# One-core layer step: the feed-forward block's weight sums and GpSimd's other arithmetic placed on VectorE

## The chip, the cores and the metric

The kernel runs on one core of one Trainium2 chip. The metric is the device time of one execution in microseconds (us). Engines are named as in the profile: PE is TensorE, DVE is VectorE, ACT is ScalarE, POOL is GpSimd, SP is SyncE (here only a DMA queue).

## The reference

One decoder layer for 512 prompt tokens and 8 sample tokens (T = 520 columns), D_MODEL = 1024, D_FF = 2816, all in 32-bit floats: RMSNorm, an input projection, an mLSTM branch and an S5 branch, a gated merge with an output projection, then the part that is changed here:

```python
x = x.astype(f32) + mix
hf = rmsnorm(x, g_ffn)
x = x + (jax.nn.silu(hf @ w_ff1) * (hf @ w_ff3)) @ w_ff2     # feed-forward block
...
y_prompt = rmsnorm(xp, norm_final_g)                         # the tail
y_sample = rmsnorm(xs, norm_final_g)
```

## The kernel before

**Three matmuls for one.** Activations stand with features on the partitions. Every weight tile is split into a high part (`w_high`, rounded by ACT, function `high` and `split_high`) and a low part (`w_low` = weights minus `w_high`, by DVE, functions `low` and `split_low`, lines 1333 and 1775). PE multiplies high by high, high by low and low by high.

**Seven products for eight.** The feed-forward block works in 17 rounds (`ROUNDS`), 11 "up" rounds (four, four and three) and after each set two "down" rounds. The tokens are two halves of 260 columns, H0 and H1, and a round takes a 2 by 2 block of weights. A Winograd scheme makes the block's product out of seven products of half size, i = 0 to 6, each computed for two output tiles (su = 0 in PSUM bank set `G`, su = 1 in `Q`). Three of its seven weight operands are blocks as loaded (`a11`, `a12`, `a22`), four are sums or differences that `sum_up(r, step)` makes in four steps on POOL: step 0 `f = f + e` (line 1249), step 1 `f = f - b` (1253), step 2 `b = e - f` (1257), step 3 `f = d - f` (1262), each over 128x1024 elements, or 128x768 in the last two rounds. `f` is `w_sums`, `b` and `d` are `raw`, `e` is `w` (tile `w_22`) or `raw`. A product has 24 matmuls (4 chunks k, three each, two su), 18 in the last two rounds.

**The seven steps of an up round on DVE and ACT.** Split units run four products ahead: `next_high(i)` on ACT needs product i to be done and rounds the weights of the product four later; `next_low(i)` on DVE makes their low part. ACT's `take(i, ...)` copies products out of PSUM into `up_a` (tile DT) and `up_b` (tile CB); semaphores `took_z0`, `took_x1`, ... tell PE that a bank is free: PE starts product 3 only after `took_x1`, product 4 after `took_x3`, 5 after `took_z0`, 6 after `took_x4`. DVE adds more products (lines 1820, 1833). POOL adds two parts (1295) and multiplies `up_b` by `ffn_rstd` (1301); DVE does the same multiplication on `up_a` (1837), takes product 6 (1840, 1843), multiplies silu(up_a) by up_b and forms differences (1846 to 1853), then writes `hidden_low` (1856, 1858). ACT may overwrite `up_a` in the next round's `take(0)` only after 1856. So each up round's end reaches PE by this chain: `hidden_low` (1856) on DVE, `take(0)`, `next_high(0)` and `take(1)` on ACT, product 3 on PE.

**Down rounds.** DVE adds each product to `x_residual` (X1, line 1870) and does `next_low(i)` behind it. Products 0 to 2 of the first down round of a set need `hidden_low` for their last chunk.

**Order of work.** Each engine's instructions stand in an order written by hand, with semaphores between engines. The SP queue loads the blocks: `load_a11(r)` waits for low part 4 of the round before, `load_a12(r)` for all sums of the round before, `load_a21` and `load_a22` for low parts 5 and 6 two rounds before.

**Entry and tail.** In the eight steps m that add the output projection to X1, POOL forms the halves' differences of the block's input (lines 1270 to 1274, into `up_a`) and adds squares (1279). At the end POOL adds squares (1313, 1318), PE sums them over the partitions, and `spread_inverse` writes the inverse root to PSUM banks 3 and 2. ACT copies bank 3 to SBUF (`inverse_copy`), from which POOL scales rows m = 5 to 7 in two instructions each (1322, 1323). DVE scales rows 0 to 4 from bank 2 in one (1895).

Of the kernel before, what the change touches and what calls it, by code (L numbers as in the profile page):

```python
# [156 lines left out]
def build(nc, wst, xt, small, apar, vbias, c0, y_o, cp_o, mp_o, s5p_o, cs_o, ns_o, ms_o, s5s_o):  # L157
# [5 lines left out]
    with ctx:  # L163
# [25 lines left out]
        cur_b = sb("cur_b", [P, 2])  # L189
# [161 lines left out]
        inv_sb = sb("inverse_copy", [P, 2, HALF], at=at_bh + 4 * T * 8)  # L351
# [96 lines left out]
        def feature(su, k):  # L448

            return 4 * k + su  # L450

# [19 lines left out]
        def _(sp):  # L471
# [23 lines left out]
            def block_of(r, row, col):  # L495

                kind, g, p = ROUNDS[r]
                if kind == "up":
                    n = N_FF + 2 * (DOWN_CUT[g] + PAIRS_OF[g] * row + p)
                    src = wst[n:n + 2]  # L500
                else:
                    n = N_DOWN + 3 * (4 * row + 2 * p) + g
                    src = wst[n:n + 4:3]
                w = P * k_of(r)
                return src.rearrange("a p n -> p a n")[:, :, w * col:w * col + w]

# [39 lines left out]
            for half, m, count in [(1, m, m + 1) for m in range(5)] + [(0, m, 6 + m) for m in range(5)]:  # L546
                sp.wait_ge(y_dve, count)
                sp.dma_start(y_o[:, m, (H0, H1)[half]], X1[:, m, (H0, H1)[half]]).then_inc(y_out, 16)

        @block.scalar  # L550
        def _(act):
# [420 lines left out]
            for count, half in enumerate((1, 0)):  # L972
                act.wait_ge(sq_summed, 2 + count + 1)
                act.activation(rt[:, 3 * half:3 * half + 3], (Q, G)[half][:, 1, 0:3], ACT.Sqrt, bias=eps[:, 0:1], scale=1.0 / D).then_inc(root_ready, 1)
                act.wait_ge(inverse_spread, 1 + count + 1)
                copy(inv_sb[:, half, :], (Q, G)[half][:, 3, 0:HALF]).then_inc(inverse_copied, 1)
            for half, m, count in [(1, m, m - 4) for m in range(5, KC)] + [(0, m, m - 1) for m in range(5, KC)]:
                act.wait_ge(y_pool, count)
                act.dma_start(y_o[:, m, (H0, H1)[half]], X1[:, m, (H0, H1)[half]]).then_inc(y_out, 16)
            act.wait_ge(y_out, 16 * 2 * KC)  # L980
        @block.gpsimd
        def _(pool):
# [259 lines left out]
            def sum_up(r, step):  # L1242

                f, b, d, e = (halves_of(x, r) for x in (FB[r % 2], BB, DB, EB[r % 2]))
                unit = N_FF + UNITS_R * r
                if step == 0:
                    pool.wait_ge(a21_in[r % 2], 16 * (r // 2) + 16)
                    pool.wait_ge(a22_in[r % 2], 16 * (r // 2) + 16)
                    tt(f, f, e, ALU.add).then_inc(sums, 1)
                elif step == 1:  # L1250
                    pool.wait_ge(a11_in, 16 * r + 16)
                    pool.wait_ge(w_lo, unit + 1)
                    tt(f, f, b, ALU.subtract).then_inc(sums, 1)  # L1253
                elif step == 2:
                    pool.wait_ge(sums, 4 * r + 2)
                    pool.wait_ge(w_lo, unit + 2)
                    tt(b, e, f, ALU.subtract).then_inc(sums, 1)
                else:
                    pool.wait_ge(sums, 4 * r + 3)
                    pool.wait_ge(a12_in, 16 * r + 16)  # L1260
                    pool.wait_ge(w_lo, unit + 4)
                    tt(f, d, f, ALU.subtract).then_inc(sums, 1)  # L1262

            for m in range(KC):
                part = DT[:, 4 * (m % 2):4 * (m % 2) + 4, :]
# [1194 lines left out]
```

## Time and profile before

| | |
|---|---|
| median of 3 runs | 1010.9 us (1008.11 to 1015.56) |
| the profiled execution | 1013.47 us, span 1011.7 us |
| granted PE clock over the span | 0.962 |
| feed-forward block and tail | from about 562 us to the end |
| DVE busy | 750.1 us |
| POOL busy | 499.2 us |

The profile comes from one execution. The span is that of its instructions, 1.8 us less than its device time. A busy time is the sum of an engine's instructions; in a timeline the bracket behind an instruction gives the engine's idle time ahead of it and what ended it.

### The profile page before, as it was taken

The page shows a single profiled execution, that of the slowest core. Times are in us where ns is not written, and L with a number is a line of the kernel's source. Part 1 is how long each engine was busy: PE and PEld are TensorE (multiplying, and loading weights), DVE is VectorE, ACT ScalarE, POOL GpSimd, SP SyncE. Part 2 cuts the span into 40 slices and gives each one's busy share as a digit, 9 for nine tenths or more (in the row PEclk, how much of TensorE's full clock was granted, in tenths as well). Part 3 has the DMA queues.
Part 4 walks back from the last instruction along what each step waited for, and adds up shares of the span by engine and source line. Part 5 has one row for each costly group of instructions (what it writes and reads, how often), then busy time and mean ns, then how long its engine had stood idle before and what let it go on. Part 6 is the DMA issues. An engine that isn't in the chain of part 4 may idle for free. (4 is left out here: it accounts for less than half of the span.)

```text
span 1011.7 us, 20752 instructions
## 1 busy us (share of the span) xinstructions
PE 925.9 (92%) x8550; PEld 890.7 (88%) x8550; DVE 750.1 (74%) x1028; ACT 509.9 (50%) x862; POOL 499.2 (49%) x512
## 2 busy tenths in 40 slices
PE   8999999999999999999999788887998887998795
PEld 4899998998998999999999688886998887998795
DVE  7879964955954967434347689998789998789893
ACT  5578377468469575233334354453444443344441
POOL 6888958246240210000016856664456664556556
PEclk9999999999999999999999998998999897999878
DMA  7423264343353345333243022222222222222112
GB/s 296 149 82 108 69 230 153 147 169 116 126 199 106 116 155 210 125 96 109 89 148 104 1 84 84 84 85 84 84 85 84 84 85 84 84 84 73 63 33 84
DMA packets 36804, 112.49 MB, mean 111 GB/s; under 512 B 3524, under 2 KB 7668, under 8 KB 34792
## 3 DMA queue, kind: packets, MB, share of 16 engines
q1 hardware_dynamic: 32032, 79.91, 23.4%
q0 software_dynamic: 2736, 24.13, 6.4%
q10 hardware_dynamic: 1944, 7.15, 2.0%
q8 instruction: 67, 1.10, 0.4%
q14 instruction: 25, 0.20, 0.1%
HBM read 97.78 MB, written 13.39 MB: 110 GB/s over the span
## 5 line engine op out<-in xcount | busy, mean ns | idle before, releaser
L554 ACT ACTIVATE w_high<-raw 128x1024 fp32r<-128x1024 f32 (+1 forms) x137 | 142.8, 1047 | 157.0 <-PE G L1921 91.2
L1333 DVE TENSOR_TENSOR w_low<-raw,w_high 128x1024 fp32r<-128x1024 f32 x78 | 98.1, 1264 | 80.5 <-ACT w_high L554 79.9
L1775 DVE TENSOR_TENSOR w_low<-raw,w_high 128x1024 fp32r<-128x1024 f32 (+1 forms) x59 | 135.1, 2289 | 27.2 <-ACT w_high L554 27.2
L2243 PE MATMUL G<-ffn_in_high,w_high 128*128 128x260 f32 x308 | 93.2, 303 | 45.0 <-ACT up_a L554 36.8
L1921 PE MATMUL G<-h_high,w_high 128*128 128x256 f32 (+1 forms) x640 | 131.1, 286 | 0.0
L1921 PE MATMUL G<-h_low,w_high 128*128 128x256 f32 (+1 forms) x640 | 129.0, 283 | 0.0
L1921 PE MATMUL G<-h_high,w_low 128*128 128x256 f32 (+1 forms) x640 | 128.9, 283 | 0.0
L2243 PEld LDWEIGHTS G<-ffn_in_high,w_high 128*128 128x128 f32 x308 | 62.7, 204 | 47.6 <-issue 43.7
L1921 PEld LDWEIGHTS G<-h_high,w_high 128*128 128x128 f32 x640 | 99.3, 188 | 2.0 <-issue 1.6
L1921 PEld LDWEIGHTS G<-h_low,w_high 128*128 128x128 f32 x640 | 99.2, 188 | 0.0
L1921 PEld LDWEIGHTS G<-h_high,w_low 128*128 128x128 f32 x640 | 99.2, 188 | 0.0
L2243 PE MATMUL G<-ffn_in_low,w_high 128*128 128x260 f32 x308 | 91.7, 298 | 0.0
L2243 PE MATMUL G<-ffn_in_high,w_low 128*128 128x260 f32 x308 | 91.7, 298 | 0.0
L1253 POOL TENSOR_TENSOR w_sums<-w_sums,raw 128x1024 f32<-128x1024 f32 (+1 forms) x17 | 41.2, 2425 | 99.7 <-DVE w_low L1775 92.9
L2243 PE MATMUL Q<-ffn_in_high,w_high 128*128 128x260 f32 x308 | 89.9, 292 | 0.0
L2243 PE MATMUL Q<-ffn_in_low,w_high 128*128 128x260 f32 x308 | 89.6, 291 | 0.0
L2243 PE MATMUL Q<-ffn_in_high,w_low 128*128 128x260 f32 x308 | 89.6, 291 | 0.0
L1262 POOL TENSOR_TENSOR w_sums<-raw,w_sums 128x1024 f32<-128x1024 f32 (+1 forms) x17 | 51.4, 3026 | 60.7 <-DVE w_low L1775 60.7
L1270 POOL TENSOR_TENSOR up_a<-x_scaled 128x260 f32<-128x260 f32 x4 | 6.6, 1638 | 141.8 <-DVE x_scaled L1787 141.8
L1775 DVE TENSOR_TENSOR w_low<-w_sums,w_high 128x1024 fp32r<-128x1024 f32 (+1 forms) x51 | 67.5, 1324 | 10.3 <-ACT w_high L554 10.1
L554 ACT ACTIVATE w_high<-w_sums 128x1024 fp32r<-128x1024 f32 (+1 forms) x51 | 52.5, 1030 | 39.3 <-PE Q L2243 32.8
L1161 POOL TENSOR_TENSOR unused_p<-unused_p 128x1 f32<-128x1 f32 x29 | 11.7, 408 | 122.0 <-PE Q L2152 30.4
(462 smaller groups left out, 2821.0 us busy)
## 6 DMA issues: line engine op xcount, KB each, us to landing
raw<-wst SPq DMA_DIRECT2D x116, 512.0 KB, 3.8
c_samples<-c POOLq DMA_DIRECT2D x4, 2048.0 KB, 8.8
out_cs<-c_samples POOLq DMA_DIRECT2D x4, 2048.0 KB, 7.9
w_sums<-wst SPq DMA_DIRECT2D x15, 512.0 KB, 4.9
v_spread<-v_scratch ACTq DMA_DIRECT2D x4, 1024.0 KB, 5.8
w<-wst SPq DMA_DIRECT2D x8, 512.0 KB, 4.4
x_tokens<-xt SPq DMA_DIRECT2D x4, 520.0 KB, 5.2
x_residual<-xt POOLq DMA_DIRECT2D x1, 2080.0 KB, 8.8
```

The lines of the kernel that those rows point to most:

```text
L554: return act.activation(out, in_, ACT.Copy, **kw)
L1161: return tt(junk_p[:, g:g + 1], junk_p[:, 0:1], junk_p[:, 0:1], ALU.mult)
L1253: tt(f, f, b, ALU.subtract).then_inc(sums, 1)
L1262: tt(f, d, f, ALU.subtract).then_inc(sums, 1)
L1270: tt(part[:, 0, :], XS[:, m, H1], XS[:, m, H0], ALU.subtract).then_inc(t_ready, 1)
L1333: tt(WL[n.slot()][:], raw[n.slot()][:], WH[n.slot()][:].bitcast(F32), ALU.subtract).then_inc(w_lo, 1)
L1775: tt(halves_of(WL[w_at(q)], r), halves_of(round_source(r, i), r), halves_of(WH[w_at(q)], r).bitcast(F32), ALU.subtract).then_inc(w_lo, 1)
L1921: last = mm(o, w[slot][:, c], h[:, k, c0_:c0_ + width], start=start and x == 0 and t == 0, stop=stop and x == n - 1 and t == 2)
L2243: last = mm((G, Q)[su][:, bank, 0:HALF], w[s][:, c], h[:, RHS[i], k, :], start=start and i < 3 and k == ks[0] and t == 0, stop=stop and k ...
```

## The change

Everything that POOL computes in the feed-forward block and the tail is issued by DVE, except for the identity matrix `ident_late`. The steps of `sum_up` stand behind the low parts: steps 0 to 3 of round r + 1 behind `next_low(r, 1)`, `(r, 3)`, `(r, 4)` and `(r, 6)`, for round 0 behind step m = 4 and low parts 0, 1 and 3. The halves' differences and sums of squares stand in DVE's loop over m. The additions of 1295 and the multiplication of 1301 stand in the up round. In the last round the squares are added behind `take(3)` and `take(4)`. `inverse_copy` and ACT's copy are gone, DVE scales all eight rows from bank 3, `spread_inverse` writes one bank, three of the nine column sums of half 0 stand earlier in PE's order, ahead of the last product's end, and ACT and SP each issue 8 of the 16 output DMAs where it was 6 and 10.

```diff
-            for r, (kind, _, _) in enumerate(ROUNDS):
-                u = up_index(r)
-                sum_up(r, 2)
-                sum_up(r, 3)
-                if r < NR - 1:
-                    sum_up(r + 1, 0)
-                    sum_up(r + 1, 1)
-                if kind == "up":
-                    for su, (p5, u3) in enumerate(((DT[:, 2, :], DT[:, 7, :]), (CB[:, 2, :], CB[:, 3, :]))):
-                        pool.wait_ge(took_z0, 2 * r + su + 1)
-                        pool.wait_ge(took_x4, 2 * r + su + 1)
-                        tt(p5, p5, u3, ALU.add).then_inc(c22_ready, 1)
...
-                    tt(CB[:, 0:3, :], CB[:, 0:3, :], frq[:, 0:3, :], ALU.mult).then_inc(b_early, 1)
...
-            for count, half in enumerate((1, 0)):
-                pool.wait_ge(inverse_copied, count + 1)
-                for m in range(5, KC):
-                    own.do(tt(X1[:, m, (H0, H1)[half]], X1[:, m, (H0, H1)[half]], inv_sb[:, half, :], ALU.mult))
-                    pool.tensor_scalar(X1[:, m, (H0, H1)[half]], X1[:, m, (H0, H1)[half]], g_fin[:, m:m + 1], None, ALU.mult).then_inc(y_pool, 1)
...
+            def sum_up(r, step):
+
+                f, b, d, e = (halves_of(x, r) for x in (FB[r % 2], BB, DB, EB[r % 2]))
+                unit = N_FF + UNITS_R * r
+                if step == 0:
+                    dve.wait_ge(a21_in[r % 2], 16 * (r // 2) + 16)
+                    dve.wait_ge(a22_in[r % 2], 16 * (r // 2) + 16)
+                    tt(f, f, e, ALU.add).then_inc(sums, 1)
+                elif step == 1:
+                    dve.wait_ge(a11_in, 16 * r + 16)
+                    dve.wait_ge(w_lo, unit + 1)
+                    tt(f, f, b, ALU.subtract).then_inc(sums, 1)
...
+            def combine_input(m):
+
+                part = DT[:, 4 * (m % 2):4 * (m % 2) + 4, :]
+                if m < 4:
+                    tt(part[:, 0, :], XS[:, m, H1], XS[:, m, H0], ALU.subtract).then_inc(t_ready, 1)
+                else:
+                    own.do(tt(part[:, 1, :], XS[:, m, H1], XS[:, m - 4, H1], ALU.subtract))
+                    own.do(tt(part[:, 2, :], part[:, 1, :], XS[:, m - 4, H0], ALU.add))
+                    tt(part[:, 3, :], XS[:, m, H0], part[:, 2, :], ALU.subtract).then_inc(t_ready, 1)
...
             def next_low(r, i):
                 if UNITS_R * r + i + 4 < UNITS_R * NR:
                     split_low(UNITS_R * r + i + 4)
+                    if r + 1 < NR and i in (1, 3, 4, 6):
+                        sum_up(r + 1, (1, 3, 4, 6).index(i))
...
                 next_low(r, 3)
+                for su, (p5, u3) in enumerate(((DT[:, 2, :], DT[:, 7, :]), (CB[:, 2, :], CB[:, 3, :]))):
+                    dve.wait_ge(took_z0, 2 * r + su + 1)
+                    dve.wait_ge(took_x4, 2 * r + su + 1)
+                    own.add(tt(p5, p5, u3, ALU.add))
                 next_low(r, 4)
...
                 tt(DT[:, 0:3, :], DT[:, 0:3, :], frq[:, 0:3, :], ALU.mult).then_inc(a_early, 1)
+                own.add(tt(CB[:, 0:3, :], CB[:, 0:3, :], frq[:, 0:3, :], ALU.mult))
                 next_low(r, 5)
...
             scale_out(1, range(3))
             invert(0)
-            scale_out(1, range(3, 5))
-            scale_out(0, range(5))
+            scale_out(1, range(3, KC))
+            scale_out(0, range(KC))
```

DVE in up round 2 before, from `next_low(2, 5)` to the end of the round (`w_low` are the low parts, `w_sums` tile `f`, `up_a` and `up_b` DT and CB, G and Q the PSUM sets):

```order
L1775 TENSOR_TENSOR w_low_55<-raw_51,w_high_52 128x1024
L1840 TENSOR_TENSOR up_a<-G,ffn_rstd 128x260
L1843 TENSOR_TENSOR up_b<-Q,ffn_rstd 128x260
L1846 TENSOR_TENSOR up_a<-up_a,up_b 128x780
L1847 TENSOR_TENSOR up_a<-up_a 128x520
L1848 TENSOR_TENSOR up_a<-up_a 128x260
L1851 TENSOR_TENSOR up_a<-up_a,up_b 128x260
L1853 TENSOR_TENSOR up_a<-up_a 128x260
L1775 TENSOR_TENSOR w_low_168<-w_sums_170,w_high_167 128x1024
L1856 TENSOR_TENSOR hidden_low<-up_a,hidden_high 128x5x260
L1858 TENSOR_TENSOR hidden_low<-up_a,hidden_high 128x2x260
```

DVE in the same round after the change, one instruction earlier in the round:

```order
L1810 TENSOR_TENSOR up_b<-up_b,ffn_rstd 128x780
L1733 TENSOR_TENSOR w_low_55<-raw_51,w_high_52 128x1024
L1813 TENSOR_TENSOR up_a<-G,ffn_rstd 128x260
L1815 TENSOR_TENSOR up_b<-Q,ffn_rstd 128x260
L1818 TENSOR_TENSOR up_a<-up_a,up_b 128x780
L1819 TENSOR_TENSOR up_a<-up_a 128x520
L1820 TENSOR_TENSOR up_a<-up_a 128x260
L1823 TENSOR_TENSOR up_a<-up_a,up_b 128x260
L1825 TENSOR_TENSOR up_a<-up_a 128x260
L1733 TENSOR_TENSOR w_low_167<-w_sums_169,w_high_166 128x1024
L1711 TENSOR_TENSOR w_sums_169<-raw_51,w_sums_169 128x1024
L1828 TENSOR_TENSOR hidden_low<-up_a,hidden_high 128x5x260
```

POOL's multiplication of `up_b` and step 3 of the sums now stand in DVE's order, the latter straight ahead of the `hidden_low` for which ACT and PE wait.

DVE at the very end, before:

```order
L1870 TENSOR_TENSOR x_residual<-x_residual,Q 128x260
L1873 TENSOR_TENSOR x_half_squares<-x_residual 128x260
L1895 SCALAR_TENSOR_TENSOR x_residual<-x_residual,gains_biases,G 128x260 x3
L1889 RECIPROCAL root_columns<-root_columns 128x3
L1895 SCALAR_TENSOR_TENSOR x_residual<-x_residual,gains_biases,G 128x260 x2
L1895 SCALAR_TENSOR_TENSOR x_residual<-x_residual,gains_biases,Q 128x260 x5
```

and after the change:

```order
L1842 TENSOR_TENSOR x_residual<-x_residual,Q 128x260
L1845 TENSOR_TENSOR x_half_squares<-x_residual 128x260
L1885 SCALAR_TENSOR_TENSOR x_residual<-x_residual,gains_biases,G 128x260 x3
L1879 RECIPROCAL root_columns<-root_columns 128x3
L1885 SCALAR_TENSOR_TENSOR x_residual<-x_residual,gains_biases,G 128x260 x5
L1885 SCALAR_TENSOR_TENSOR x_residual<-x_residual,gains_biases,Q 128x260 x8
```

DVE scales 8 rows of each half where it scaled 5; POOL's twelve instructions for the other three rows are gone.

## Rows read from the trace of the kernel before

**Rows 1.** The page: busy time, share of the span and instruction count of each engine.
```profile
PE 925.9 (92%) x8550; PEld 890.7 (88%) x8550; DVE 750.1 (74%) x1028; ACT 509.9 (50%) x862; POOL 499.2 (49%) x512
```

**Rows 2.** Stretch, length, PE, PEld, DVE, ACT, POOL busy, PEclk, DMA; up, then down.
```profile
664.00:688.40 24.40, 19.76 (x151) 19.56 (x151) 23.32 (x22) 10.78 (x15) 14.88 (x8) 0.92 0.25 88
715.00:735.00 20.00, 19.52 (x163) 19.34 (x163) 14.92 (x18) 7.57 (x11) 10.01 (x5) 1.00 0.32 106
```

**Rows 3.** PE's timeline: start, length, instruction, and the idle time before it.
```profile
580.68 0.36 PE L2243 MATMUL G<-ffn_in_high,w_high 128*128 128x260 f32 x1 [3.27 <-issue]
586.27 0.56 PE L2243 MATMUL G<-ffn_in_high,w_high 128*128 128x260 f32 x1 [2.48 <-ACT up_a L554]
611.03 0.56 PE L2243 MATMUL G<-ffn_in_high,w_high 128*128 128x260 f32 x1 [5.93 <-ACT up_a L554]
663.97 0.36 PE L2243 MATMUL G<-ffn_in_high,w_high 128*128 128x260 f32 x1 [4.74 <-ACT up_a L554]
688.39 0.58 PE L2243 MATMUL G<-hidden_high,w_high 128*128 128x260 f32 x1 [4.64 <-DVE hidden_low L1856]
694.92 0.53 PE L2243 MATMUL G<-hidden_high,w_high 128*128 128x260 f32 x1 [2.61 <-DVE x_residual L1870]
761.63 0.36 PE L2243 MATMUL G<-ffn_in_high,w_high 128*128 128x260 f32 x1 [3.64 <-ACT up_a L554]
```

**Rows 4.** Waits from 590 us on: who for whom, us in total, times, longest.
```profile
PE G L2243 <- ACT up_a L554: 34.3, 8, 5.9
...
PE G L2243 <- DVE hidden_low L1856: 14.2, 3, 4.8
...
POOL w_sums L1253 <- DMA raw<-wst: 6.8, 1, 6.8
```

**Rows 5.** One operation, w_low from raw: ns min, median, max, ahead of (L1333) and within (L1775) the feed-forward block; landings.
```profile
L1333 DVE TENSOR_TENSOR w_low<-raw,w_high x78: 1210/1226/1759, 15.1 to 547.6; 128x1024 fp32r<-128x1024 f32 x78
L1775 DVE TENSOR_TENSOR w_low<-raw,w_high x59: 948/2374/3439, 555.8 to 981.3; 128x1024 fp32r<-128x1024 f32 x52, 128x768 fp32r<-128x768 f32 x7
...
DMA to landing us min/median/max: 3.1/3.8/9.1
```

**Rows 6.** DVE's timeline in round 2, an up round.
```profile
651.33 2.90 DVE L1775 TENSOR_TENSOR w_low<-raw,w_high 128x1024 fp32r<-128x1024 f32 x1
654.15 0.42 DVE L1840 TENSOR_TENSOR up_a<-G,ffn_rstd 128x260 f32<-128x260 f32 x1
654.49 0.41 DVE L1843 TENSOR_TENSOR up_b<-Q,ffn_rstd 128x260 f32<-128x260 f32 x1
654.82 2.52 DVE L1846 TENSOR_TENSOR up_a<-up_a,up_b 128x780 f32<-128x780 f32 x1
657.38 0.70 DVE L1847 TENSOR_TENSOR up_a<-up_a 128x520 f32<-128x520 f32 x1
...
659.27 1.22 DVE L1775 TENSOR_TENSOR w_low<-w_sums,w_high 128x1024 fp32r<-128x1024 f32 x1
660.40 1.51 DVE L1856 TENSOR_TENSOR hidden_low<-up_a,hidden_high 128x1300 fp32r<-128x1300 f32 x1
661.83 2.85 DVE L1858 TENSOR_TENSOR hidden_low<-up_a,hidden_high 128x520 fp32r<-128x520 f32 x1
664.60 3.40 DVE L1775 TENSOR_TENSOR w_low<-raw,w_high 128x1024 fp32r<-128x1024 f32 x1
```

**Rows 7.** POOL's timeline in the same stretch.
```profile
653.10 3.42 POOL L1257 TENSOR_TENSOR raw<-raw,w_sums 128x1024 f32<-128x1024 f32 x1
660.65 3.47 POOL L1262 TENSOR_TENSOR w_sums<-raw,w_sums 128x1024 f32<-128x1024 f32 x1 [4.14 <-DVE w_low L1775]
```

**Rows 8.** ACT's timeline in the same stretch.
```profile
668.93 1.05 ACT L554 ACTIVATE w_high<-w_sums 128x1024 fp32r<-128x1024 f32 x1
```

**Rows 9.** Last POOL and DVE instructions of the tail, from two timelines.
```profile
1008.12 0.93 POOL L1323 TENSOR_SCALAR x_residual<-x_residual,gains_biases 128x260 f32<-128x260 f32 x1
...
1002.29 2.07 DVE L1895 SCALAR_TENSOR_TENSOR x_residual<-x_residual,gains_biases,Q 128x260 f32<-128x260 f32 x5 [0.89 <-PE Q L2319]
```

More of the change, by code:

```diff
@@ L545, in _ @@
                 load_a12(r)
-            for half, m, count in [(1, m, m + 1) for m in range(5)] + [(0, m, 6 + m) for m in range(5)]:
-                sp.wait_ge(y_dve, count)
+            for half, m in [(half, m) for half in (1, 0) for m in range(0, KC, 2)]:
+                sp.wait_ge(y_dve, KC * (1 - half) + m + 1)
                 sp.dma_start(y_o[:, m, (H0, H1)[half]], X1[:, m, (H0, H1)[half]]).then_inc(y_out, 16)
@@ L974, in _ @@
                 act.activation(rt[:, 3 * half:3 * half + 3], (Q, G)[half][:, 1, 0:3], ACT.Sqrt, bias=eps[:, 0:1], scale=1.0 / D).then_inc(root_ready, 1)
[L975 to L978, printed above, removed]
+            for half, m in [(half, m) for half in (1, 0) for m in range(1, KC, 2)]:
+                act.wait_ge(y_dve, KC * (1 - half) + m + 1)
                 act.dma_start(y_o[:, m, (H0, H1)[half]], X1[:, m, (H0, H1)[half]]).then_inc(y_out, 16)
@@ L1240, in _ @@
             pool.wait_ge(x1_in, 16)
[L1242 to L1262, printed above, removed]
@@ L1881, in down_round, with add_whole_squares, add_half_squares @@
                 take(3, x, 0, H1, took_x3)
+                if last:
+                    add_whole_squares(range(1, 4))
                 take(4, x, 1, H1, took_x4, took_z0)
+                if last:
+                    add_half_squares(range(4))
                 take(5, 2, 0, H1, took_z5, took_x3)
                 take(6, x, 1, H0, took_x6)
+            def add_whole_squares(ks):
+                for i in ks:
+                    dve.wait_ge(sq_ready, 2 * KC + i + 1)
+                    if i > 1:
+                        dve.wait_ge(sq_added, 1 + KC + i - 1)
+                    tt(facc[:], sqf[0][:] if i == 1 else facc[:], sqf[i][:], ALU.add).then_inc(sq_added, 1)
+            def add_half_squares(ks):
+                for i in ks:
+                    part = facc[:, (H0, H1)[i // 2]]
+                    dve.wait_ge(sq_ready, 2 * KC + 4 + i + 1)
+                    dve.wait_ge(sq_added, 1 + KC + 3 + i)
+                    tt(part, part, sqh[i][:], ALU.add).then_inc(sq_added, 1)
             def invert(half):
@@ L2316, in spread_inverse @@
                 pe.wait_ge(inverse_ready, 3 + 2 - half)
-                for bank in (3, 2):
-                    for j, (_, w) in enumerate(FIN_TILES):
-                        last = mm((Q, G)[half][:, bank, P * j:P * j + w], rt[:, 3 * half + j:3 * half + j + 1].broadcast_to([P, P]),
-                                  ident_late[:, P - w:P], start=True, stop=True)
+                for j, (_, w) in enumerate(FIN_TILES):
+                    last = mm((Q, G)[half][:, 3, P * j:P * j + w], rt[:, 3 * half + j:3 * half + j + 1].broadcast_to([P, P]),
+                              ident_late[:, P - w:P], start=True, stop=True)
                 last.then_inc(inverse_spread, 1)
@@ L2325, in _ @@
             spread_inverse(1)
-            sum_squares(0)
+            sum_squares(0, range(1, 3))
             spread_inverse(0)
```

127 lines of the change are left out of this document (57 added, 70 removed).

## The prediction, written before the result

> **What bounds the kernel now.** I read the busy times first, then the stretches, then PE's gaps, then the two vector engines side by side. Over the span PE is busy 925.9 us and DVE 750.1 [rows 1], which would make PE the bound. By stretch it is otherwise. In down rounds PE is busy 19.5 of 20 us and DVE 14.9, in an up round DVE 23.3 of 24.4 and PE 19.8 [rows 2]. The reader is to see there that what this change is worth is decided in 11 up rounds, by DVE. PE's gaps say where: once per up round PE stops ahead of product 3 (611.03, 663.97, 761.63) or, if a down round follows, ahead of its last chunks (688.39), for 3.6 to 5.9 us [rows 3]; those stops make up 34.3 + 14.2 us [rows 4]. From 611.03 to 663.97 are two up rounds, 26.5 us each, where PE's own work is 20.2 (163 matmuls in 19.52 us are 0.12 each [rows 2], 24 a product 2.9, seven products).
>
> Why DVE is full is in rows 5 to 7. The same operation on 128x1024 elements takes 1.23 us at the median ahead of the block (78 of them) and 2.37 within it (59) [rows 5]. In one up round it takes 1.22 us at 659.27, where POOL is idle, and 2.90 at 651.33 and 3.40 at 664.60, where POOL works [rows 6, 7]. The others that read two SBUF tiles suffer too: 2.52 us for 780 elements at 654.82 and 2.85 for 520 at 661.83, which takes 0.70 at 657.38. The one at 654.15, inside POOL's instruction but with PSUM as one input, takes its usual 0.42. So DVE stands still while a POOL instruction on SBUF runs. These four rows alone hold 1.7 + 2.2 + 1.6 + 2.2 = 7.6 us above their clean prices.
>
> **Clean prices.** 1024 elements 1.21 us, 1.13 from start to start if nothing is waited for (659.27 to 660.40), 1.25 if the next instruction waits for it; 520 elements 0.70; 260 elements 0.42, 0.34 from start to start (654.15 to 654.49); 1300 elements 1.51 [rows 6]. For 780 elements no row is clean: between 0.70 (520) and 1.21 (1024) the line gives 0.96, bounds are 0.70 and the 2.52 shown; I take 0.96, 0.88 from start to start. By the formula in the Trainium skill's page VectorE: DVE Perf Modes, section on the TRN2 errata, an fp32 tensor_tensor takes (N + 151)/0.96 ns, which is 1.22 us for 1024, as measured, and 0.97 for 780; the sum would not move.
>
> **The up round.** The change puts on DVE four sums of 1.13 to 1.25, two additions of 0.35 and one multiplication of 0.88, 6.4 us in all, and takes away the standing still. DVE's clean work is then 7 low parts and 4 sums (12.9 us with three waits for its own result), 8 short ones from PSUM or for `up_b` (2.7), two multiplications by `ffn_rstd` (1.8), the block from line 1846 to 1853 (1.0 + 1.89 from 657.38 to 659.27) and `hidden_low` (2.0): 22.3 us. That is above PE's 20.2, so DVE stays the bound, and what counts is the chain. Let time 0 be PE's start of product 3 (663.97). ACT's rounding for `next_low(3)` ends at 668.93 + 1.05, that is 6.0 [rows 8], that for `next_low(4)` one product later, at 8.9; both hang on PE's products, which the change leaves where they are. DVE has six instructions to do before that, from about -0.4 on (two low parts, step 0, two additions, a third low part, 5.2 us and 0.6 of waiting for ACT), so it starts `next_low(3)` at 6.0. From there it never waits: low part and step 1 2.39, two additions 0.70, low part and step 2 2.39, two additions 0.68, two multiplications 1.84, low part 1.14, two from product 6 0.68, block 2.89, low part and step 3 2.39, `hidden_low` 1.51. Sum 16.6, end at 22.6. From the end of 1856 (661.91) to PE's start (663.97) are 2.06 us through ACT. So the next product 3 starts at 24.7, where it was 26.5: **1.75 us** for each up round whose predecessor is an up round or whose successor is a down round (24.42 before at 688.39, 22.6 after). There are eight such intervals: 14 us. PE still idles about 3 us in each.
>
> What the moves cost elsewhere. Step 3 stands ahead of 1856, 1.2 us on the chain, counted above. ACT waits for step 2 before `next_high(0)` and step 3 before `next_high(1)` of the next round; both are done ahead of 1856, so nothing. Behind a `sum_up` that waits for a block, the whole of DVE is queued, and PE and ACT behind it. The tightest is step 1: its block a11 is asked for when low part 4 is done (about 0.8) and needed at 7.3, with landings of 3.8 us at the median and 9.1 at most [rows 5]. I take zero; if all came last it would be 2.6 us a round.
>
> **The other stages.** (a) Entry. PE's wait ahead of product 3 of round 0, 3.27 us [rows 3], comes from POOL's steps 1 and 2 late in ACT's order; on DVE they are made two steps m earlier, and product 3 can start behind product 2, 3.1 us sooner. DVE pays for it: its loop over m = 5 to 7 grows by three short instructions (1.3), a squares addition (0.65) and one or two sums each, and saves the wait for POOL's three. By my count the last x1 and PE's product 1 come half a microsecond later, which PE makes good in product 2, where it waits for DVE's low part of the input before and after. The next gap (2.48 at 586.27) shrinks to 0.6, as ACT is no longer behind step 3. Together 5.2 us; bounds 2 and 7. (b) From there to product 3 of round 1 were 24.8 us; the chain above with the reciprocal of round 0 in it gives 23.2: 1.6 us. (c) First down round of a set: PE waited 2.61 us more at 694.92, because DVE stood still in the second `hidden_low` and in a low part. Both clean save 3.6 us on DVE; but `take(3)` then comes behind a low part and step 0, and PE, which wants it 1.45 us after product 3's G half, waits about 1.8 at product 4. Net 2.1, twice, and 0.6 in the last set with its smaller blocks: 4.8. (d) Down rounds: DVE 11 x 1.17 + 14 x 0.34 = 17.6 us against PE's 20.2, hidden; its cover is the 2.6 us left, and where that is gone each microsecond costs one. In the last two rounds it is 14.3 against 15.2. (e) First up round of sets 2 and 3: the wait at 761.63 falls from 3.64 to 3.0, and half a microsecond of short waits goes: 2.2 for both. (f) Tail. POOL's last scaling ended at 1009.05, DVE's at 1004.36 [rows 9]. DVE now does all, at 0.41 each (five in 2.07), so three more in each half. Those of the second half add 1.2 us, those of the first fall mostly into the 0.89 that DVE waited ahead of its last five and add 0.3; PE writes one bank for two, three matmuls or 0.4 us less in each half. DVE ends at 1004.36 + 1.5 - 0.8 = 1005.1, 4.0 before POOL did. The squares on DVE delay its last additions by about 1 us and spare PE the wait for POOL's, even; about 1 us goes as the last low parts are clean and `take(3)` comes in time. Together **5 us**, and what follows the last scaling (1013.5 less 1009.05) stays.
>
> Sum: 14 + 5.2 + 1.6 + 4.8 + 2.2 + 5.0 = 33 us. The profiled execution took 1013.5 us, 2.6 above the median of the runs, so it becomes 980.5 and the median 1010.9 becomes **978 us**. Its own range is 970 to 988.
>
> **Rivals.** (A) The slow DVE rows are slow for another reason, ACT's or the DMAs' traffic, and stay slow. Place: every up round. DVE gets 6.4 us more and has 1.1 idle [rows 2], so each of 11 rounds grows by 5.3 us: +58, less 5 in the tail, some **1065 us, slower**. It decides if less than 6.4 us a round goes away. Against it: the four rows with 7.6 us above clean price, each under a POOL instruction. For it: they are also under ACT's and PE's instructions. Chance 0.04. The Trainium skill's Perfetto Trace Analysis, section Optimizing Scalar/DVE Operations, says that with DVE saturated it may make sense to offload some work to GpSimd, the reverse of this change; it adds that the two share an SBUF read port, so that it might not help, and [rows 5 to 7] speak for the addition. (B) In-order waits on DVE take back half: blocks that land late ahead of step 1 (up to 2.6 us x 11 = 28), or `take(3)` late in all six down rounds (1.8 x 6 = 11). Middle 17: **995 us**. For it: one sum waited 6.8 us for its block already [rows 4]. Chance 0.15. (C) More is gained: the floor is DVE's 22.3 us of work a round, not 24.7, if ACT comes sooner where PE does; 2.4 x 8 = 19 at most, half of it 10, and with the entry at its upper bound **966 us**. For it: PE's granted clock is 0.92 in the up stretch and 1.00 in the down one [rows 2], and with shorter stops it may stay up. Chance 0.12. (D) Nothing changes because the bound was PE after all (20 of 24.4 us): 1011, chance 0.02.
>
> **How the numbers follow.** My forecast has 0.67. The range leaves out A, D, and the outer part of B and C: 963 to 995. A measurement here can tell about 1% (10 us) from no change, as the runs of before lie 7 us apart. Faster by over 1% (under 1001): forecast, C, and most of B, 0.92. Within 1%: D and the rest of B, 0.04. Slower: A, 0.04.
>
> **What would show it.** w_low's median in the block at 1.21 to 1.23 us and no DVE instruction of 520 elements above 0.8; up rounds 24.7 us apart with PE idle about 3 us ahead of product 3; DVE busy some 90% in up rounds; down rounds at 20.2; DVE's last scaling the last instruction of all engines, some 4 us before the end. Wrong would be: waits of DVE for DMA ahead of step 1, PE waiting for `x_residual` in each down round, or DVE rows above 2 us with POOL idle.

## The result, and the profile after

The changed kernel takes **980.85 us** (median of 4 runs, 978.18 to 983.21), the kernel before 1009.81 on the same chip: a ratio of 0.9703, 95% interval 0.9656 to 0.975 (the quotient of these two medians is 0.9713). The profiled execution took 980.57 us, 978.8 of them span, 32.9 less than the one before.

The busy line of the page, against [rows 1]:

```profile
PE 916.1 (94%) x8538; PEld 881.6 (90%) x8538; DVE 736.9 (75%) x1165; ACT 507.9 (52%) x860; POOL 205.2 (21%) x369
```

294 us left POOL. DVE has 137 instructions more and is busy 13 us less: the 68 sums alone are some 80 us of new work (below), so over 90 us of standing still went away. A busy time of the profile counts a moment in which two instructions overlap once, so it is not quite their sum: DVE's instructions of the first interval below add up to 23.9 us within it, and its busy time is 22.31.

Five stretches (columns as in [rows 2]): two whole up intervals, 20 us of down rounds, and the 3.5 us behind PE's restart in each of the two intervals:

```profile
627.61:651.83 24.22, 20.37 (x168) 20.20 (x169) 22.31 (x29) 12.62 (x20) 0.00 (x0) 0.96 0.27 87
770.54:796.52 25.98, 23.03 (x169) 22.86 (x169) 22.40 (x29) 12.61 (x21) 0.00 (x0) 0.89 0.24 81
700.00:720.00 20.00, 20.00 (x167) 19.82 (x166) 16.61 (x21) 8.09 (x11) 0.00 (x0) 1.00 0.29 104
627.60:631.00 3.40, 3.39 (x28) 3.40 (x29) 3.12 (x3) 2.56 (x5) 0.00 (x0) 1.00 0.39 122
770.50:774.00 3.50, 3.46 (x16) 3.49 (x17) 3.22 (x4) 2.45 (x4) 0.00 (x0) 0.50 0.44 117
```

DVE is busy 22.3 to 22.4 us in an up round. In the 20 us of down rounds PE does not idle, and DVE has 3.4 us left. The two up intervals hold the same work, yet one is 1.76 longer. The last two lines show where they part: the granted clock behind the restart was 1.00 in one and 0.50 in the other, the lower level of 1.2 GHz, in which PE got 16 matmuls done instead of 28.

PE's starts behind its stops, against [rows 3]:

```profile
602.68 0.56 PE L2233 MATMUL G<-ffn_in_high,w_high 128*128 128x260 f32 x1 [3.99 <-ACT up_a L552]
627.61 0.36 PE L2233 MATMUL G<-ffn_in_high,w_high 128*128 128x260 f32 x1 [3.18 <-ACT up_a L552]
...
675.66 0.39 PE L2233 MATMUL G<-hidden_high,w_high 128*128 128x260 f32 x1 [3.26 <-DVE hidden_low L1828]
684.23 0.36 PE L2233 MATMUL G<-hidden_high,w_high 128*128 128x260 f32 x1 [1.63 <-DVE x_residual L1842]
770.54 0.56 PE L2233 MATMUL G<-ffn_in_high,w_high 128*128 128x260 f32 x1 [3.13 <-ACT up_a L552]
```

611.03 of before is 602.68 here, 688.39 is 675.66. The stop at 684.23, ahead of product 4 of the first down round, is new. Two rows of the kernel before, for two readings below: the start of that product 4, and the stretch behind the restart at 663.97:

```profile
699.40 0.28 PE L2243 MATMUL G<-hidden_high,w_high 128*128 128x260 f32 x1
...
663.97:667.50 3.53, 3.53 (x17) 3.53 (x18) 3.53 (x2) 2.53 (x4) 2.94 (x2) 0.54 0.02 5
```

The clock was low behind most restarts of the kernel before too. Its up-to-up intervals were 26.43 to 26.53 us all the same, whether the clock of the first 3.4 us was 0.50 (from 788.08) or 1.00 (from 761.63).

Waits from 560 us on, against [rows 4]:

```profile
DVE w_low L1733 <- ACT w_high L552: 33.6, 43, 1.7
...
PE G L2233 <- ACT up_a L552: 26.6, 8, 4.0
...
PE G L2233 <- DVE hidden_low L1828: 10.5, 3, 4.0
...
PE G L2233 <- DVE x_residual L1842: 5.7, 6, 1.6
```

In the kernel before the last of these was:

```profile
PE G L2243 <- DVE x_residual L1870: 7.5, 6, 2.6
```

The two waits that made up 48.5 us are 37.1. PE waits 5.7 us for `x_residual` where it was 7.5; the larger part has moved from product 3 to product 4. No wait of DVE for a DMA is among the groups listed.

The operation of [rows 5], within the block:

```profile
L1733 DVE TENSOR_TENSOR w_low<-raw,w_high x59: 951/1220/1227, 556.8 to 952.7; 128x1024 fp32r<-128x1024 f32 x52, 128x768 fp32r<-128x768 f32 x7
```

Its median is 1.22 us where it was 2.37, its longest 1.23 where it was 3.44. In DVE's timeline, full-clock interval, against [rows 6]:

```profile
632.81 1.22 DVE L1733 TENSOR_TENSOR w_low<-w_sums,w_high 128x1024 fp32r<-128x1024 f32 x1
634.13 1.22 DVE L1702 TENSOR_TENSOR w_sums<-w_sums,raw 128x1024 f32<-128x1024 f32 x1
...
639.31 0.97 DVE L1809 TENSOR_TENSOR up_a<-up_a,ffn_rstd 128x780 f32<-128x780 f32 x1
...
642.89 0.96 DVE L1818 TENSOR_TENSOR up_a<-up_a,up_b 128x780 f32<-128x780 f32 x1
...
648.26 1.51 DVE L1828 TENSOR_TENSOR hidden_low<-up_a,hidden_high 128x1300 fp32r<-128x1300 f32 x1
649.68 0.70 DVE L1830 TENSOR_TENSOR hidden_low<-up_a,hidden_high 128x520 fp32r<-128x520 f32 x1
```

The 780-element operation takes 0.96 to 0.97 us, the value that was chosen between two sizes, `hidden_low` of 520 elements 0.70 instead of 2.85, and a sum costs 1.22. ACT's rounding ahead of the low part at 632.81, and the same three places in the interval with the low clock:

```profile
631.18 1.06 ACT L552 ACTIVATE w_high<-w_sums 128x1024 fp32r<-128x1024 f32 x1
...
776.12 0.39 ACT L552 ACTIVATE up_b<-Q 128x260 f32<-128x260 f32 x1 [2.21 <-PE Q L2233]
776.40 1.05 ACT L552 ACTIVATE w_high<-w_sums 128x1024 fp32r<-128x1024 f32 x1
...
777.48 1.23 DVE L1733 TENSOR_TENSOR w_low<-w_sums,w_high 128x1024 fp32r<-128x1024 f32 x1 [1.66 <-ACT w_high L552]
```

At full clock ACT's rounding ends 4.6 us behind PE's start of product 3 (631.18 + 1.06 - 627.61) and DVE doesn't wait for it. At 776.12 ACT had waited 2.21 us for a product that PE made at half speed; the rounding ends 6.9 us behind the start, and DVE waits 1.66. That is the interval's 1.76.

The last two rows of the tail, against [rows 9]:

```profile
971.23 2.04 DVE L1885 SCALAR_TENSOR_TENSOR x_residual<-x_residual,gains_biases,G 128x260 f32<-128x260 f32 x5
973.19 3.25 DVE L1885 SCALAR_TENSOR_TENSOR x_residual<-x_residual,gains_biases,Q 128x260 f32<-128x260 f32 x8
```

All eight rows of half 0 are scaled in 3.25 us. DVE ends at 976.4, no engine computes after it, and the span ends 2.4 us later.

### The profile page after: what moved, and what is told of

The parts are those of the page before. It is cut to its first block, busy times and chain, and to the rows that moved or that the text cites. A ratio compares the mean times of both kernels' runs of the same rounds, so it can differ in the third digit from the quotient of the medians.

```text
span 978.8 us, 20691 instructions
## 1 busy us (share of the span) xinstructions
PE 916.1 (94%) x8538; PEld 881.6 (90%) x8538; DVE 736.9 (75%) x1165; ACT 507.9 (52%) x860; POOL 205.2 (21%) x369
## 4 chain that ended last, share of the span: by engine, by line
PE 57%; DVE 23%; issue 7%; POOL 7%; ACT 4%; DMA 0%; DVEq 0%; ACTq 0%; SPq 0%; POOLq 0%
PE G L1911 27%; PE G L2233 9%; PE Q L2233 8%; DVE w_low L1733 5%; PE G L2001 4%; POOL pool_tmp L984 3%; PE Q L1911 2%; ACT w_high L552 2%; DVE hidden_low L1828 2%; DVE w_sums L1711 1%; DVE up_a L1809 1%; DVE up_a L1818 1%; DVE up_b L1810 1%; DVE c_samples L1519 1%; PE Q L2059 1%
## 5 line engine op out<-in xcount | busy, mean ns | idle before, releaser
L2233 PE MATMUL G<-ffn_in_high,w_high 128*128 128x260 f32 x308 | 92.1, 299 | 31.1 <-ACT up_a L552 26.6
L1733 DVE TENSOR_TENSOR w_low<-raw,w_high 128x1024 fp32r<-128x1024 f32 (+1 forms) x59 | 70.2, 1189 | 13.2 <-ACT w_high L552 13.2
L1733 DVE TENSOR_TENSOR w_low<-w_sums,w_high 128x1024 fp32r<-128x1024 f32 (+1 forms) x51 | 60.8, 1192 | 20.1 <-ACT w_high L552 19.9
L2233 PEld LDWEIGHTS G<-ffn_in_high,w_low 128*128 128x128 f32 x308 | 62.0, 201 | 0.0
L2233 PEld LDWEIGHTS G<-ffn_in_low,w_high 128*128 128x128 f32 x308 | 61.9, 201 | 0.0
L2233 PE MATMUL G<-hidden_high,w_high 128*128 128x260 f32 x154 | 45.8, 298 | 16.3 <-DVE hidden_low L1828 10.5
```

Source lines behind the costliest of these rows:

```text
L1733: tt(halves_of(WL[w_at(q)], r), halves_of(round_source(r, i), r), halves_of(WH[w_at(q)], r).bitcast(F32), ALU.subtract).then_inc(w_lo, 1)
L2233: last = mm((G, Q)[su][:, bank, 0:HALF], w[s][:, c], h[:, RHS[i], k, :], start=start and i < 3 and k == ks[0] and t == 0, stop=stop and k ...
```

## The experiments

The first three ask what makes DVE stand still, the next three divide the change, the last six look for what bounds the up round now. All ratios are to the kernel before.

**GpSimd instructions that read.** Put into the changed kernel, on a tile that nobody uses, with nobody waiting for them:

```diff
+            def idle_work(r):
+                for i in (1, 3, 4, 6):
+                    pool.wait_ge(su_done, 2 * (UNITS_R * r + i) + 2)
+                    for _ in range(2):
+                        own.do(tt(idle[:], idle[:], idle[:], ALU.add))
```

> The changed kernel, with nothing of its work taken off DVE, and idle work added on GpSimd: behind products 1, 3, 4 and 6 of rounds 0 to 14 two tensor_tensor additions each of 480 elements, which read and write a scratch tile that nobody else uses. Port theory (DVE stands still while a GpSimd instruction reads SBUF): DVE instructions with two SBUF inputs stretch again, those with a PSUM input do not, up rounds go from about 24.7 us to 28 to 32, the time to 1010 to 1060 us. Rival (the gain of the change came from fewer handovers between engines and a better order of the sums): GpSimd waits for others and nobody waits for it, so 981 us, within 5.

1036.13 us (1033.24 to 1038.32), ratio 1.0255 (1.0229 to 1.0281): 55 us above the changed kernel, from 120 instructions that no result depends on. POOL's and DVE's timelines at one of the places:

```profile
609.56 6.83 POOL L1243 TENSOR_TENSOR idle_work<-idle_work 128x480 f32<-128x480 f32 x4 [4.49 <-PE Q L2243]
...
610.01 0.42 DVE L1798 TENSOR_TENSOR up_b<-Q,up_b 128x260 f32<-128x260 f32 x1
610.35 1.34 DVE L1743 TENSOR_TENSOR w_low<-raw,w_high 128x1024 fp32r<-128x1024 f32 x1
611.61 2.00 DVE L1743 TENSOR_TENSOR w_low<-w_sums,w_high 128x1024 fp32r<-128x1024 f32 x1
613.72 1.82 DVE L1712 TENSOR_TENSOR w_sums<-w_sums,raw 128x1024 f32<-128x1024 f32 x1
615.47 1.21 DVE L1810 TENSOR_TENSOR up_a<-up_a 128x260 f32<-128x260 f32 x1
...
616.94 1.21 DVE L1743 TENSOR_TENSOR w_low<-raw,w_high 128x1024 fp32r<-128x1024 f32 x1
```

While POOL works, the additions of two SBUF tiles take 1.34, 2.00, 1.82 and 1.21 us (the last is of 260 elements, 0.42 elsewhere); the one with a PSUM input keeps 0.42, and the low part at 616.94, which starts when POOL is done, has its 1.21. DVE's busy time is 793.4 us, 56.5 more than 736.9, and the kernel is 55.3 slower: nearly every microsecond that DVE stood still is in the time.

**GpSimd instructions that only write.** The same places, five memsets of 480 elements in each instead of two additions:

```diff
-                    for _ in range(2):
-                        own.do(tt(idle[:], idle[:], idle[:], ALU.add))
+                    for _ in range(5):
+                        own.do(pool.memset(idle[:], 0.0))
```

> The same idle work on GpSimd, but as memsets of 480 elements, five in place of two, which write SBUF and read nothing. If only the read side is shared: DVE rows keep their 1.22 us and the time stays at 981 us, within 5. If any GpSimd access to SBUF stops DVE: w_low rows stretch, over 995 us.

982.93 us (980.77 to 983.27), ratio 0.9716 (0.9691 to 0.9741): nothing. From 600 to 660 us, grouped by form:

```profile
L1243 POOL MEMSET idle_work<- 128x480 f32 x45 | 22.5, 501 | 40.0 <-PE Q L2243 37.8
...
L1743 DVE TENSOR_TENSOR w_low<-w_sums,w_high 128x1024 fp32r<-128x1024 f32 x8 | 9.8, 1224 | 4.0 <-ACT w_high L553 4.0
```

300 instructions, 0.50 us each, and the low part stays at 1.22. So it is neither POOL being busy nor its semaphores, and not ACT or the DMAs, whose work was the same in both. The Trainium skill's page SBUF — State Buffer, section Who interferes with whom, says just this: a DVE instruction with two SBUF inputs contends with a GpSimd instruction that reads SBUF, not with one that only writes it. The two runs agree.

**GpSimd instructions that read one tile.** The additions replaced by multiplications of the tile by a constant:

```diff
-                    for _ in range(2):
-                        own.do(tt(idle[:], idle[:], idle[:], ALU.add))
+                    for _ in range(3):
+                        own.do(pool.tensor_scalar(idle[:], idle[:], 1.0, None, ALU.mult))
```

> The changed kernel plus idle work on GpSimd in the same 60 places as the run with GpSimd reads, but each instruction multiplies one SBUF tile of 480 elements by a constant (one input instead of two), three times in each place instead of twice. Theory port: any GpSimd instruction that reads SBUF holds up DVE's two-input instructions, one-input ones too: then with 180 instructions of 0.5 to 0.8 us the kernel takes 1000 us or more and DVE's rows above 1.4 us come back. Rival: only two-input GpSimd instructions hold DVE up, as the memsets, which read nothing, did not: then 979 to 984 us with DVE's rows at 1.21 to 1.23.

1011.1 us (1007.79 to 1012.28), ratio 0.9988 (0.9973 to 1.0003), 30 above the changed kernel. Rows of DVE from 590 to 1000 us, and POOL's instruction (ns at least, median, most):

```profile
L1838 DVE TENSOR_TENSOR hidden_low<-up_a,hidden_high 128x1300 fp32r<-128x1300 f32 x11 | 19.7, 1790 | 0.0
...
L1820 DVE TENSOR_TENSOR up_b<-up_b,ffn_rstd 128x780 f32<-128x780 f32 x11 | 14.9, 1351 | 0.0
...
L1243 POOL TENSOR_SCALAR idle_work<-idle_work x180: 1407/1508/2350, 570.1 to 955.6; 128x480 f32<-128x480 f32 x180
```

`hidden_low` 1.79 us on the mean instead of 1.51, the 780-element multiplication 1.35 instead of 0.96. One input is enough. DVE's busy time grew by 33.4 us for 180 instructions, 0.19 us for each, where the two-input ones cost 0.47.

**The sums back on POOL**, everything else as changed:

```diff
             def sum_up(r, step):
-                    dve.wait_ge(a21_in[r % 2], 16 * (r // 2) + 16)
+                    pool.wait_ge(a21_in[r % 2], 16 * (r // 2) + 16)
...
+            for r in range(NR):
+                sum_up(r, 2)
+                sum_up(r, 3)
...
-                    if r + 1 < NR and i in (1, 3, 4, 6):
-                        sum_up(r + 1, (1, 3, 4, 6).index(i))
```

> The changed kernel with the sums of weight blocks alone back on GpSimd; additions and multiplication in the up rounds, entry and tail stay on DVE. Port theory: the sums are most of GpSimd's reading, DVE loses 4.7 us a round of its own work and stands still again in low parts and hidden_low; rounds come back near 26 us, entry keeps part and the tail all of its gain: 1000 to 1008 us. Handover rival (what cost was the path through GpSimd's lines 1295 and 1301): 978 to 988 us.

994.46 us (994.0 to 997.61), ratio 0.9846 (0.9819 to 0.9873). Page and PE's starts:

```profile
PE 921.2 (93%) x8538; PEld 885.5 (89%) x8538; DVE 763.5 (77%) x1097; ACT 509.0 (51%) x860; POOL 385.7 (39%) x437
...
629.81 0.36 PE L2239 MATMUL G<-ffn_in_high,w_high 128*128 128x260 f32 x1 [3.92 <-ACT up_a L552]
655.52 0.56 PE L2239 MATMUL G<-ffn_in_high,w_high 128*128 128x260 f32 x1 [3.85 <-ACT up_a L552]
```

Up intervals are 25.7 us. DVE has 68 instructions fewer than after the change and is busy 26.6 us longer. The 68 sums are 60 of 1.22 and 8 of 0.96 on DVE, 81 us in all, so with them on POOL DVE stood still for 26.6 + 81 = 107.5 us: **1.58 us of standing still for each sum, against 1.19 for making it itself.** This counts a sum by its duration; counted by the 1.14 us from its start to the next instruction's, it would be 1.50 against 1.11. The time is 5 us below the range on record: the share of the sums in the gain was overestimated there.

**Only the sums on DVE**, POOL keeps the rest (the kernel before with this and `sum_up` in DVE's program):

```diff
                     split_low(UNITS_R * r + i + 4)
+                    if r + 1 < NR and i in (1, 3, 4, 6):
+                        sum_up(r + 1, (1, 3, 4, 6).index(i))
```

> The kernel before with the sums of weight blocks alone on DVE; additions, multiplication, entry and tail stay on GpSimd. Port theory: GpSimd keeps 4.9 us of reading in an up round (1295 and 1301) and the tail its 4 us, DVE stands still for some 2.5 us a round: 990 to 1000 us. Handover rival: 1005 to 1015 us.

1002.86 us (1001.19 to 1003.74), ratio 0.9916 (0.9891 to 0.994). Two up intervals and two instructions of DVE:

```profile
605.00:631.31 26.31, 22.37 (x168) 22.18 (x169) 23.34 (x26) 12.61 (x20) 5.10 (x3) 0.89 0.25 81
631.31:658.05 26.74, 22.81 (x168) 22.63 (x169) 23.33 (x26) 12.61 (x20) 5.10 (x3) 0.88 0.25 79
...
638.22 1.23 DVE L1766 TENSOR_TENSOR w_low<-w_sums,w_high 128x1024 fp32r<-128x1024 f32 x1 [1.63 <-ACT w_high L554]
...
645.61 2.91 DVE L1766 TENSOR_TENSOR w_low<-raw,w_high 128x1024 fp32r<-128x1024 f32 x1
```

The time is 3 us above the range on record. The up intervals gained nothing (26.3 and 26.7), and what was won is in the entry (product 3 of round 1 at 605.00) and at the first down rounds (9.25 us instead of 11.01 from the last chunks to product 4). DVE took the sums on, but the multiplication of `up_b` on POOL still holds up a low part (645.61), and behind a low clock another one waits 1.63 for ACT (638.22). Sums alone bring 8 us, the rest without the sums 16.5, both together 30: more than the two added.

**Only the tail**, in the kernel before: `inverse_copy` and POOL's scaling gone, one bank written.

```diff
-            scale_out(1, range(3, 5))
-            scale_out(0, range(5))
+            scale_out(1, range(3, KC))
+            scale_out(0, range(KC))
```

> The kernel before with the tail alone changed: DVE scales all eight rows of each half from PSUM bank 3, ACT's copy and GpSimd's twelve scalings are gone, one bank is written, output DMAs split 8 and 8. Sums, squares, additions and entry stay on GpSimd. By the prediction's tail term, 3 to 4 us less than before: 1006 to 1008 us. If the stores, not the scaling, set the end: within 1 us of before.

1007.73 us (1006.2 to 1009.03, 6 runs) beside 1012.25: 0.9949 (0.9931 to 0.9967), or 4.5 us. The squares stay on POOL here, and the column sums in their old place.

**Step 3 of the sums later.** In up rounds it is moved behind both `hidden_low`, off the chain that reaches PE:

```diff
-                    if r + 1 < NR and i in (1, 3, 4, 6):
+                    if r + 1 < NR and i in ((1, 3, 4) if ROUNDS[r][0] == "up" else (1, 3, 4, 6)):
...
                 tt(HIDL[:, 5:7, k, :], DT[:, 6:8, :], HIDH[:, 5:7, k, :].bitcast(F32), ALU.subtract).then_inc(hidl_ready, 1)
+                sum_up(r + 1, 3)
```

> The changed kernel with step 3 of the sums behind both hidden_low instructions of an up round instead of ahead of them; nothing else. Chain theory (an up round's length is set by DVE's work between product 3 and the first hidden_low, and DVE has 1.06 us idle behind the second): each interval loses 1.2 us, 24.5 becomes about 23.3, and the 11 stops together 13 us: 966 to 971 us. Rival, DVE's total of work sets the round: nothing changes, 981 us, as DVE executes the same instructions.

961.81 us (960.38 to 964.06), ratio 0.9506 (0.9482 to 0.9529): 19 us faster than the changed kernel and 4 below the range on record. A sum of 1.15 us off the chain in 11 up rounds accounts for 13. PE's starts:

```profile
624.47 0.36 PE L2234 MATMUL G<-ffn_in_high,w_high 128*128 128x260 f32 x1 [1.73 <-ACT up_a L552]
647.32 0.36 PE L2234 MATMUL G<-ffn_in_high,w_high 128*128 128x260 f32 x1 [2.47 <-ACT up_a L552]
```

The interval is 22.85 us, 1.37 less than the full-clock interval of the changed kernel and 3.1 less than its longest; one of five is 23.65. The stops are 1.7 to 2.6 us where they were 3 to 4, and the clock over the span is 0.987 instead of 0.973.

**Step 0 later too**, behind `take(3)` in down rounds, so that PE needn't wait at product 4:

```diff
-                    if r + 1 < NR and i in ((1, 3, 4) if ROUNDS[r][0] == "up" else (1, 3, 4, 6)):
+                    if r + 1 < NR and i in ((1, 3, 4) if ROUNDS[r][0] == "up" else (3, 4, 6)):
...
+                    if i == 3 and not last:
+                        sum_up(r + 1, 0)
```

> As the kernel with step 3 late, and in the down rounds step 0 of the next round's sums stands behind take(3) in place of ahead of take(2). If PE's 1.3 to 1.6 us ahead of product 4 in each first down round come from step 0 in DVE's order, they go: 3 to 4 us below the kernel with step 3 late. If they come from ACT's rounding: equal to it.

962.76 us (961.05 to 964.06), ratio 0.9505 (0.9481 to 0.9528): a miss. PE's wait at product 4 fell from 1.63 to 0.50 us, which is 1.1 us less in each set. But four of the five up-to-up intervals are 23.6 to 23.7 us and not 22.85. The stretch behind a stop of 1.81 us at 736.83, and DVE a little later:

```profile
736.80:740.00 3.20, 3.17 (x16) 3.20 (x17) 2.92 (x3) 2.44 (x4) 0.00 (x0) 0.55 0.38 99
...
742.88 1.23 DVE L1733 TENSOR_TENSOR w_low<-w_sums,w_high 128x1024 fp32r<-128x1024 f32 x1 [0.78 <-ACT w_high L552]
```

Again the clock is low behind the stop (0.55), and DVE waits 0.78 for ACT where it did not wait in the run before. There a stop of the same 1.81 us, ahead of 736.76, was followed by a clock of 1.00. Why it fell here and not there stays open.

**ACT's `take(1)` ahead of `next_high(0)`**, first with steps 3 and 0 moved as above, then with step 3 alone:

```diff
                 take(0, 2, 2, took_z0)
-                next_high(0)
                 take(1, x, 1, took_x1)
+                next_high(0)
                 next_high(1)
```

> As the kernel with step 0 late too, and ACT in an up round does take(1) ahead of next_high(0). Chain theory: from hidden_low to PE's product 3 are 2.06 us, of which next_high(0) is 1.0; a round loses up to 1 us more until PE's own 20.2 to 21.6 us bind: 6 to 9 us below the kernel with step 0 late. Rival, the low part of product 4 now comes late and PE waits there for DVE: no change.

959.01 us (958.47 to 959.73), ratio 0.9469 (0.9447 to 0.949), and an up interval of:

```profile
600.59:623.64 23.05, 20.86 (x169) 20.33 (x169) 22.12 (x29) 12.42 (x21) 0.00 (x0) 1.00 0.27 92
```

The clock is at 1.00 in all five, DVE busy 22.12 of 23.05 us. The gain over the run before is 3.8 us, where 6 to 9 were expected.

> The changed kernel with the two reorderings that helped: step 3 of the sums behind both hidden_low in up rounds, and ACT's take(1) ahead of next_high(0), but step 0 left in its place behind low part 1. Theory: DVE's own work of 22.3 us bounds the up round and take(1) adds the same 3 us as it did with step 0 moved: 957 to 960 us, intervals near 22.6 to 23.0. Rival: with step 0 early, product 4 of the down rounds waits 1.6 us again, and the rest is as before, so 960 to 963. If moving take(1) helped only in the company of the moved step 0: 961.8.

961.23 us (960.89 to 962.04), ratio 0.9493 (0.9464 to 0.9522). Its intervals are 23.05 us too, 0.2 longer than the 22.85 of step 3 alone, and its time the same as that one's within what the runs spread. The range on record, 957 to 960, was missed by 1 us. What `take(1)` buys seems to be the clock: with step 0 moved, where four intervals had 23.6 to 23.7, it brings 3.8 us, without it 0.6. Seen the other way, moving step 0, a miss by itself, is worth 2.2 us (959.01 against 961.23) once the clock stays at 1.00. An up interval of 23 us is 0.9 above DVE's own 22.1.

**PE's stops filled.** In the changed kernel, ahead of product 3 of up rounds and of the last chunks of first down rounds, matmuls whose result nobody reads:

```diff
+            def fill(r):
+                pe.wait_ge(took_x6, 2 * r)
+                for _ in range(10):
+                    mm(G[:, 3 - bank_x(r), 0:P], ones[:], ones[:], start=True, stop=True)
```

> The changed kernel plus ten extra matmuls of 128 columns on a constant tile (some 2.0 to 2.5 us of PE work, results unread) placed where PE stops in the up rounds: ahead of product 3 of every up round that follows an up round, and ahead of the first chunk that needs hidden_low in the first down round of a set. They wait only for a PSUM bank, so they run inside the stop. Theory clock: in the changed kernel the granted clock falls after some stops, products 3 and 4 then come late for ACT's takes, and that is why intervals of 24.9 to 26.0 us stand beside some of 23.1 to 24.2. With PE busy through the stop the clock stays up, the long intervals become 23.1 to 24.2, and the kernel takes 974 to 978 us, with a granted clock of 0.98 or more. Theory order: the spread of the intervals is from DVE's and ACT's waits for each other and the clock only follows; then nothing is gained: 980 to 983. If the filling outlasts a stop, or delays a matmul of product 3, up to 0.5 us a round is lost, 986 at most.

973.32 us (971.46 to 974.48), ratio 0.9616 (0.9586 to 0.9646): more work, 7.5 us less time. The stretch, then the filling (each matmul is two records) and PE's start behind it:

```profile
602.04:626.25 24.21, 22.64 (x188) 22.45 (x188) 22.29 (x29) 12.58 (x20) 0.00 (x0) 1.00 0.26 87
...
597.99 2.39 PE L2257 MATMUL G<-ones 128*128 128x128 f32 x20
602.04 0.39 PE L2233 MATMUL G<-ffn_in_high,w_high 128*128 128x260 f32 x1 [1.66 <-ACT up_a L552]
```

The stop is as long as before, 4.05 us from 597.99 to 602.04, but 2.39 of it are filled, the clock is 1.00, and all five up-to-up intervals are 24.21 or 24.22 us, where the changed kernel had 24.93, 24.22, 25.08, 25.98 and 24.90. The eight intervals sum to 185.8 us instead of 192.1. Hence in the changed kernel the low clock behind a stop costs 6.3 us in the up rounds, by the chain shown above (PE's late product, ACT, DVE).

**The same filling in the kernel before**, with the same edit as above.

> The kernel before (sums and the rest on GpSimd) with the same ten extra matmuls in each stop of the up rounds as in the filled version of the changed kernel. There the filling took 7.5 us off and made every interval 24.22 us. In the kernel before, the intervals between up rounds are 26.43 to 26.53 us whether the granted clock over them was 0.89 or 0.98, so DVE's held-up instructions, not PE's late products, should set them. Theory: the clock is on the chain only once DVE's stalls are gone; filling gives 0 to 2 us here, 1008 to 1012 us, intervals unchanged. Rival: the clock costs the kernel before as much as the changed one, and the filling gives 5 to 8 us, 1003 to 1006 us; then part of the change's own gain was smaller than the clock's swings make it look.

1013.4 us (1009.39 to 1014.44), ratio 1.0004 (0.9987 to 1.0021). PE's starts are 26.4 us apart, as without it:

```profile
636.93 0.39 PE L2243 MATMUL G<-ffn_in_high,w_high 128*128 128x260 f32 x1 [0.84 <-ACT up_a L554]
663.35 0.39 PE L2243 MATMUL G<-ffn_in_high,w_high 128*128 128x260 f32 x1 [0.84 <-ACT up_a L554]
```

With DVE held up, PE's late products were covered. The clock came onto the chain only with this change.

## Why the prediction was right

It gave 978 us (963 to 995) by 33 us less in the profiled execution; 32.9 were measured. That they agree to 0.1 us is luck, as single terms are off by up to 1.5 us in both directions; that the time fell into the range is not. The median came out 2.9 higher, at 980.85: I had set the 2.6 us by which the profiled execution of before lay above its median against the one after, and that one lay at its own. By its own terms, from the starts of PE in both traces:

| term | predicted | measured |
|---|---|---|
| entry and round 0, (a) and (b), to product 3 of round 1 | 6.8 | 8.35 |
| eight up intervals | 14 | 12.55 |
| (c) first down rounds of sets 1 and 2, to product 4 | 4.2 | 2.4 + 2.3 |
| (e) to the first up round of sets 2 and 3 | 2.2 | 1.0 + 0.9 |
| (c) last set and (f) what follows its product 4, the tail | 0.6 + 5.0 | 1.2 + 4.1 |
| sum | 32.8 | 32.9 |

**Entry.** (a), to product 4 of round 0 (586.27 before, 579.54 after), came to 6.7 us where 5.2 were put; 0.3 of them lie ahead of the changed part. (b) was put at 1.6 us and is 1.6.

**DVE stands still for POOL's reads.** Shown by the three runs with idle work, and by a sum that costs DVE 1.58 us on POOL and 1.19 on itself. Rival (A) falls.

**The up round.** DVE's own work was put at 22.3 us and is 22.3 to 22.4. From the end of `hidden_low` to PE's start I took 2.06 us from before, and the trace has 2.06 again. The chain came to 24.7 us; at full clock it is 24.2, as ACT's rounding ends 4.6 us behind PE's start and not 6.0, so that DVE starts `next_low(3)` at 5.2, when its own work is done, instead of 6.0. From there to the end of `hidden_low` it takes 17.0 us, where 16.6 were summed: the durations held to 0.01 us, but a low part with its sum takes 2.46 to 2.49 and not 2.39. What the sum lacked is the clock: four of the five up-to-up intervals are 0.7 to 1.8 us above 24.2. I had taken ACT's 6.0 from one interval and made it hold for all; that interval ran at 0.54 behind its start (the row of 663.97 above), so a part of the clock's price was in it unnoticed. The five came to 7.25 us of gain against 8.75. The three ahead of a down round gained 0.6, 1.3 and 3.4 us against 1.8 each, which happens to give the same sum. The errors leave 1.45 of 14 us: sizes, not steps.

**Moved waits.** PE's wait at product 4 was put at 1.8 us and measured 1.63, 1.28 and 0.75. DVE waits nowhere for a block ahead of step 1, and PE's waits at product 4 come in the first down round of a set alone, not in all six, so rival (B) did not come. Rival (C) had a clock that stays up with shorter stops and the floor of 22.3 us. The change alone did not get there; filled stops gave the clock, and the reordering 22.85 us.

**The parts aren't a sum.** Sums alone would have brought 8 us and the rest 16.5. The prediction costed the whole at once by the chain of one round, and this is why it held: the gains of the two halves, each measured alone, add up to 24.5 of some 30.

**The tail.** 5 us predicted, 4.5 measured alone, 4.1 in the changed kernel by the table.

## What to carry to other kernels

Look at one operation's durations by what GpSimd does at the time before crediting it with taking work off VectorE: here each offloaded sum cost VectorE more than making it. Once such a change has put one engine on the chain, walk the chain again: the one sum that stood ahead of `hidden_low` without need was worth 19 us more, two thirds of the change itself. A stop of TensorE can cost more than its length, if the products behind it feed the engine that bounds.

## What the runs showed of the hardware

- A GpSimd instruction that reads one SBUF tile holds VectorE's two-input instructions up as well, 0.19 us of VectorE's busy time for each of 180, against 0.47 for each of 120 that read two; 300 memsets cost it nothing (737.3 us busy against 736.9).
- The granted clock behind a stop is not settled by the length of the stop: behind 3.18 us it was 1.00, behind 3.13 it was 0.50 for 3.5 us, and with shorter stops it was 0.55 behind one of 1.81 and, in another run, 1.00 behind one of the same 1.81. What decides stays open. With the stops filled but for 0.8 to 1.8 us it was 1.00 in the up intervals.
- Extra TensorE work made the kernel 7.5 us faster where it kept the clock at 1.00, and did nothing where another engine covered the loss.
